# A decoder layer on one core: latents, queries, keys and values computed span by span inside the tail program

## What is computed

```python
h = rmsnorm(x)                                   # width 1024
b_g, c_g, x_in, q_lat, kv_lat, kr_raw, gate_c, gate_a = split(h @ w_in)
conv_y = short_conv(c_g * x_in)                  # width 512, 3 taps
# latents and queries: the part that is moved
ckv = rmsnorm(kv_lat); kr = apply_rope(rmsnorm(kr_raw))          # 256 and 32 wide
q   = rmsnorm(q_lat) @ w_uq                                      # 384 -> 8 heads x 96
qn  = rmsnorm(q[..., :64]); qr = apply_rope(rmsnorm(q[..., 64:]))
kn  = rmsnorm(ckv @ w_uk); v = ckv @ w_uv                        # 8 heads x 64
# the rest
attn = softmax(qn.kn + qr.kr) @ v
x = x + (sigmoid(gate_c) * (b_g*conv_y) @ w_conv_out + sigmoid(gate_a) * attn @ w_attn_out) @ w_mix_out
h = rmsnorm(x)
# PEER: 8 heads, 2 x 128 keys each, top 16 of the pairs -> 128 experts (of 16384) per token
a = gelu(sum(u[eidx] * h)); x = x + sum(softmax(best) * a * v[eidx])
```

## Time and profile before

| | us |
|---|---|
| median of the runs (3914.68 to 3929.59) | 3915.71 |
| profiled execution: its own time | 3925.3 |
| profiled execution: its span, first to last instruction | 3923.5 |
| latent and query stage (from 46.6 to 370.0) | 323.4 |
| span 0 in the tail (370.0 to the first gather at 719.3) | 349.3 |
| gathers of span 0, beside the work of span 1 (to 1526.6) | 807.3 |
| gathers of span 1, beside the work of span 2 (to 2627.4) | 1100.8 |
| gathers of span 2, beside the work of span 3 (to 3824.1) | 1196.7 |
| gathers of span 3 | 99.4 |

### The profile page before, as it was taken

How to read it: one execution, slowest core, us unless ns; L and a number is a source line. 1 busy time by engine, 2 the same in 40 slices (tenths; PEclk the granted TensorE clock), 3 DMA queues, 4 the chain that set the end, 5 groups by cost and what they waited for, 6 DMA issues and landing times.

```text
span 3923.5 us, 36349 instructions
## 1 busy us (share of the span) xinstructions
PE 3260.3 (83%) x10704; PEld 1824.9 (47%) x10704; DVE 2617.0 (67%) x5677; ACT 1405.3 (36%) x4207; POOL 1120.7 (29%) x1252
## 2 busy tenths in 40 slices
PE   6797898488999987777888899877788887787887
PEld 4423787245555443344544454423444444575431
DVE  1364117777757996777687779964777676756874
ACT  1122201485123233666522233333454444222343
POOL 0000001333323333333333334342333333323442
PEclk9897799788999999888899999998888988676899
DMA  2112243699999989999999999998898888999999
GB/s 92 33 36 67 91 150 102 259 399 404 397 364 408 363 316 372 411 407 406 376 426 426 426 414 378 377 389 344 325 368 350 338 360 336 391 401 412 425 421 385
DMA packets 234020, 1289.23 MB, mean 329 GB/s; under 512 B 45468, under 2 KB 59868, under 8 KB 98341
## 3 DMA queue, kind: packets, MB, share of 16 engines
q0 software_dynamic: 152064, 1107.36, 69.5%
q1 hardware_dynamic: 80036, 175.22, 12.6%
q10 hardware_dynamic: 1728, 4.39, 0.3%
HBM read 1273.47 MB, written 13.40 MB: 328 GB/s over the span
## 4 chain that ended last, share of the span: by engine, by line
PE 35%; DMA 27%; DVE 16%; ACT 5%; issue 5%; POOL 1%; SPq 1%; ACTq 0%; DVEq 0%; POOLq 0%
DMA tl_uv<-in_uv,tl_idx 23%; PE tl_y L905 12%; PE tl_f L1151 6%; DVE tl_uv L1490 3%; PE tl_f L1131 3%; PE tl_f L1162 3%; DVE tl_acc L1477 2%; PE tl_f L1177 2%; DMA X<-in_krope 2%; PE tl_f L965 1%; PE tl_f L1075 1%; PE tl_f L1098 1%; DVE tl_eq L1574 1%; POOL tl_uv L837 1%; PE tl_f L1017 1%
## 5 line engine op out<-in xcount | busy, mean ns | idle before, releaser
L1490 DVE CUSTOM_DVE_ANT_0 tl_uv<-tl_uv,tl_h 128x1024 f32<-128x1024 f32 x1056 | 1272.4, 1217 | 706.4 <-DMA tl_uv<-in_uv,tl_idx 680.4
L837 POOL DMA_INDIRECT tl_uv<-in_uv,tl_idx x1056 | 1042.4, 987 | 1941.1 <-PE tl_y L905 1378.7
L905 PE MATMUL tl_y<-tl_uv,tl_diag 128*128 128x512 f32 (+1 forms) x2552 | 1318.6, 659 | 254.9 <-ACT tl_diag L1198 254.8
L905 PEld LDWEIGHTS tl_y<-tl_uv,tl_diag 128*128 128x128 f32 (+1 forms) x2552 | 491.0, 204 | 916.5 <-issue 497.9
L1226 ACT ACTIVATE tl_ge<-tl_a 128x1 f32<-128x1 f32 x1056 | 209.0, 198 | 1248.1 <-DVE tl_a L1490 1246.5
L1477 DVE SCALAR_TENSOR_TENSOR tl_acc<-tl_uv,tl_w,tl_acc 128x1024 f32<-128x1024 f32 x410 | 524.9, 1280 | 67.2 <-ACT tl_w L1210 66.5
L1210 ACT ACTIVATE tl_w<-tl_ge,tl_weight 128x1 f32<-128x1 f32 x1024 | 301.5, 294 | 33.2
L849 POOL TENSOR_TENSOR tl_cand<-tl_tv 128x48 f32<-128x48 f32 (+5 forms) x128 | 66.1, 544 | 784.2 <-DVE tl_ti L1522 626.1
L1151 PE MATMUL tl_f<-H,w_tail 128*128 128x384 f32 (+2 forms) x1024 | 266.0, 417 | 11.6 <-DMA w_tail<-in_w_merge 7.7
L1177 PE MATMUL tl_f<-H,w_tail 128*128 128x384 f32 (+2 forms) x1024 | 265.8, 414 | 10.2 <-DVE H L1717 9.6
L1198 ACT ACTIVATE tl_diag<-K,tl_w 128x128 f32<-128x128 f32 (+1 forms) x638 | 253.6, 397 | 34.4 <-PE tl_y L905 14.1
(11 more groups left out here) (213 smaller groups left out, 3119.4 us busy)
## 6 DMA issues: line engine op xcount, KB each, us to landing
w_tail<-in_w_merge SPq DMA_DIRECT2D x96, 512.0 KB, 7.6
w_tail<-in_w_peer SPq DMA_DIRECT2D x64, 576.0 KB, 7.7
w_tail<-in_w_conv SPq DMA_DIRECT2D x48, 512.0 KB, 7.9
tl_uv<-in_uv,tl_idx POOLq DMA_INDIRECT x1056, 11.4
w_tail<-in_w_mix SPq DMA_DIRECT2D x32, 512.0 KB, 7.6
X<-in_cache SPq DMA_DIRECT2D x64, 128.0 KB
X<-in_x SPq DMA_DIRECT2D x8, 536.0 KB, 6.9
o_y<-tl_acc ACTq DMA_DIRECT2D x8, 512.0 KB, 6.3
```

The costliest lines, as they stand in the source:

```text
L837: pool.indirect_dma_start(UV[:, u % RING, :], None, d["uv"], bass.IndirectOffsetOnAxis(ap=which, axis=0)).then_inc(landed[u % RING], 16)
L905: mm = pe.matmul(Y[0:m, half * 512:(half + 1) * 512], DG[:, (pe_count[u] - 1) % DIAGS, 0:m], UV[:, u % RING, D + half * 512:D + (half + 1) ...
L1490: dve.tensor_tensor_reduce(UV[:, u % RING, 0:D], UV[:, u % RING, 0:D], HP[:], 1.0, 0.0, ALU.mult, ALU.add, A[:, t % 2, i:i + 1]).then_inc( ...
```

## The change

`latent_stage` and `query_stage` are gone, with the loads ahead of them. Their work stands at the head of each span in `tail_stage`, for that span's tokens alone (272, 384, 384, 32; the meta tokens go with span 0):

- `project(c)`: the six latent blocks for the span's tokens, as six more groups of the weight ring (fetched again in each span), the sums of squares by matmul, roots, reciprocals, scaling and RoPE of KR.
- `questions(c)`: for each tile of 128 tokens (and once for the meta tokens) queries, keys and values with tokens on the partitions. Then a head's sum of squares is a DVE reduction along the free axis, and its reciprocal root a number per token and head, used straight from SBUF. The matmuls for sums and spreads of the query stage go; transposes of q and k by PE (per tile 16 of them) come in, because attention wants channels on the partitions. `w_uq`, `w_uk` and `w_uv` are loaded in each span, the first two into the weight ring's space.
- Queries, keys and values of a tile are still stored to HBM, tile by tile, and attention of the same span reads them back after waiting for these stores.
- The `TICK` table gets entries for the new steps (8 ticks each, for 8 + 3 x tiles + 2 steps; 6 for span 3's projection), so units are spread over them too.
- The samples' absorbed queries stay in SBUF, and the decode's loads are issued a little later in the span.

The core of the diff (removed functions and equal edits of offsets left out):

```diff
-                            norm_stage(nc, "n1_", X, H, K, d["g_mix"], w_lat, x_dram=d["x"])
-                            latent_stage(nc, H, K, CQ, CKV, KR, CS, w_lat, w_head, out_kept, d)
-                        query_stage(nc, K, CQ, CKV, KR, CS, QABS, QRS, w_head, out_kept, d)
+                norm_stage(nc, "n1_", X, H, K, d["g_mix"], w_tail, x_dram=d["x"])
                 tail_stage(nc, K, X, H, w_tail, d)
...
         for c in range(NCH):
+            order += [(c, LATENT, b) for b in range(4)] + [(c, LSUM, 0), (c, LATENT, 4), (c, LATENT, 5), (c, LSUM, 1), (c, LSUM, 2)]
+            for z in range(len(steps[c])):
+                order += turn_groups(c, z - 1) * (z > 0)
+                order += [(c, QP, 2 * z), (c, QP, 2 * z + 1)] * asks(c, z) + [(c, KP, z), (c, VP, z)] * keeps(c)
...
-        PRE = [len(x) + 5 + NCV for x in items] + [DEC + NCV]
-        TICK = [[6 + 2 * PARTS[c][1]] * len(items[c]) + [8] * 5 + [8] * NCV
+        BODY = [len(x) + 5 + NCV for x in items] + [DEC + NCV]
+        ASK = [3 * len(x) + 2 for x in steps]
+        PRE = [BODY[c] + ASK[c] + NLT + 2 for c in range(NCH)]
+        TICK = [[8] * (NLT + 2) + [8] * ASK[c]
+                + [6 + 2 * PARTS[c][1]] * len(items[c]) + [8] * 5 + [8] * NCV
...
@@ SyncE
+            def ask_loads(c):
+                p0, n = lat_span[c]
+                sp.wait_ge(proj, ready[c, LATENT, NLT - 1])
+                sp.dma_start(WQ, d["w_uq"]).then_inc(wq_in, 16)
...
+                    sp.dma_start(WK, d["w_uk"]).then_inc(wq_in, 16)
+                    sp.dma_start(WV[:], d["w_uv"]).then_inc(wq_in, 16)
...
+                for z, (lo, m, t) in enumerate(steps[c] if keeps(c) else []):
+                    sp.wait_ge(act_took, act_count[c, KTR, 2 * z + 1])
...
+                        sp.dma_start(d["s_q"][:, :, t * P:(t + 1) * P].rearrange("h p n -> p h n"), QTT[:]
+                                     ).then_inc(q_stored, 16)
+                    sp.dma_start(d["s_k"][:, :, at:at + m].rearrange("h p n -> p h n"), KTT[:, :, 0:m]).then_inc(q_stored, 16)
...
             def attention_loads(c, a, n):
-                if c:
-                    sp.wait_ge(proj, ready[c - 1, SCORE, HC - 1])
-                    sp.wait_ge(ranked, c)
+                sp.wait_ge(lat_stored, 32 * (c + 1))
+                sp.wait_ge(q_stored, 16 * kept(c + 1, 0))
...
@@ TensorE
+            def project(c):
...
+                for b in range(NLT):
+                    units(due(c, b - PRE[c], 0))
...
+                    for k in range(KD):
+                        mm = pe.matmul(F[0:m, bank_of[c, LATENT, b], 0:n], W[:, s, k, 0:m], H[:, k, p0:p0 + n],
+                                       start=(k == 0), stop=(k == KD - 1))
...
+            def ask(c, z):
+                lo, m, t = steps[c][z]
+                if z == 0:
+                    pe.wait_ge(wq_in, 16 * (3 * c + (3 if keeps(c) else 1)))
+                    pe.wait_ge(lat_set, c + 1)
...
+            def ask_turn(c, z):
+                m = steps[c][z][1]
+                if asks(c, z):
+                    pe.wait_ge(q_norm, asked(c, z) + 1)
...
+            def questions(c):
+                n, at = len(steps[c]), ASK[c] + BODY[c]
+                for z in range(n + 1):
+                    units(due(c, 3 * z - at, 0))
+                    if z:
+                        ask_turn(c, z - 1)
+                    if z < n:
+                        ask(c, z)
...
@@ ScalarE
+            def ask_root(c, z):
...
+                act.wait_ge(q_ss, at_step(c, z) + 1)
+                ins = act.activation(QRT[0:m, a:b], QSS[0:m, a:b], ACT.Sqrt, bias=K[0:m, C_EPS:C_EPS + 1], scale=1.0 / NOPE)
...
@@ VectorE
+            def project(c):
+                n, at = lat_span[c][1], 8 * c
+                units(due(c, NLT - PRE[c], LAG_DVE))
...
+                dve.wait_ge(lat_root, c + 1)
+                for i, (b0, b1) in enumerate(((0, QT), (QT, QT + KT), (QT + KT, NLT))):
...
+                    dve.reciprocal(r, r).then_inc(lat_step, 1)
+                    dve.wait_ge(lat_step, at + i + 1)
+                    for b in range(b0, b1):
+                        x = LQ[:, b, 0:n] if b < QT else LC[:, b - QT, 0:n] if b < NLT - 1 else LR[:, 0:n]
+                        ins = dve.scalar_tensor_tensor(x, x, GLAT[0:m, b:b + 1], r, ALU.mult, ALU.mult)
...
+            def questions(c):
+                at = ASK[c] + BODY[c]
+                for z in range(len(steps[c])):
+                    units(due(c, 3 * z - at, LAG_DVE))
+                    ask_squares(c, z)
+                    units(due(c, 3 * z + 1 - at, LAG_DVE))
+                    ask_scale(c, z)
```

More of the change, by code:

```diff
@@ L501, in start, with load @@
         sp.dma_start(self.tile[:, s, 0:src.shape[1], :], src).then_inc(self.arrived[s], 16)
+    def load(self, sp):
+        for w in range(WRING):
+            self.start(sp, w)
 def tail_stage(nc, K, X, H, weights, d):
```

727 lines of the change are left out of this document (351 added, 376 removed).

## The result

The changed kernel takes 3952.77 us (median of 7 runs, 3948.66 to 3962.62), the kernel before 3917.11 in the same series (7 runs, 3914.68 to 3932.64): a ratio of 1.0088, 95% interval [1.0069, 1.0106]. It is slower by 0.9%, where the prediction said 2.0% faster. The profiled execution has a span of 3955.5 us against 3923.5.

The account below looks back on a forecast made before the run. Engines one by one bound it before the first gather; after, engines in span 1, DMA in span 2. 3923.5 - 240 + 89 + 42 + 30 = 3844.5, + 1.8 - 9.6, said 3836 us; over all cases 3750 to 3898.

Parts of the forecast that it names:

- The front: Up to the first gather: two stages of 323.4 us go, 89 us of work comes back; 240 us earlier.
- Bytes: Traffic added beside the units in spans 1 and 2: 8.6 MB, 20 us, or 26 with small stores at half rate.
- Span 1: Gather 0 to 256: new steps cost 153 us, 52 returned elsewhere, 12 at the stream's start; net +89 us.
- Span 2: Gather 256 to 640: new steps cost 150 us, units moved out of old ones return 108; net +42 us.
- the DMA needs 47 x 2.43 + 26 = 140: it sets the pace: Span 2's new steps: 47 units at 2.43 us plus 26 us of bytes exceed PE's 124 us; 140 us.
- returned 47 units at 2.3: 108: Span 2's old stretches: 47 units now stand in new steps, each giving back 2.3 us; 108 us.
- 8 buffers (19 us of gathers) cover waits of 6 to 13 us: Span 2's new steps: landed gathers outlast PE's waits, so DMA keeps the pace; 19 us of gathers.
- Span 3: Gather 640 to 1024: new steps cost 87 us, less 20 units at 2.5 and 7 at the start; net +30 us.
- The table loads: On ACT, ten more roots between GELUs bring 20 loads of 1.28 us, 26 us, costing nothing beyond the chains' counted loads.
- the 3862: Whole-kernel time if each table load on ACT also drained about 1.38 us, 28 us more; left out of the sum.
- A: Only bytes count beside the units: added PE and DVE work finds room, 64 us come back, 3740 us; 17%, below 3785.
- B: New steps: ring closes, units hide nothing, serial length 347 us, 4023 us; decides from 240 exposed; 9%, above 3935.

Follow-up runs that it names:

- experiment 2: Kernel before, with 17 extra DRAM-to-DRAM copies (8.8 MB) in each of spans 1 and 2 and no engine work: 3957.11 us, ratio 1.0111.
- Experiment 1: Kernel before, with 20/25 in place of 23/25 of the units beside span 2's work spread over it, no new steps: 3966.54 us, ratio 1.0134.
- experiment 7: Changed kernel, with no units in the new steps of spans 1 to 3: 3956.38 us, ratio 1.0112.
- experiment 8: Changed kernel, with 24 ticks in place of 8 ahead of the first tile and of attention: 3920.70 us; with 48: 3926.77 us.
- experiment 10: Spread share 24 of 25 for 23: kernel before 3932.18, changed 3894.97, changed with gathered units 3857.67 us; 25 of 25: before 3937.49, gathered 3891.16.
- experiment 3: Changed kernel, with attention of spans 1 and 2 reading an input without waiting for the stores, which are still made: 3950.48 us, ratio 1.0093.
- experiment 4: Changed kernel, with q, k, v of spans 1 and 2 not stored and attention reading an input: 3927.52 us, ratio 1.0024.
- experiment 5: Changed kernel, storing values in rows of 2 KB: 3954.66 us; storing q, k and v in rows of 2 to 4 KB: 3964.0 us.

## Why the prediction was wrong

**The front** was right: 240 us forecast, 242 measured (scores at 135.5 for 136, first gather at 477.3 for 479).

**Bytes** were right in size: 20 us a span forecast for the bytes as such, 19.2 and 20.5 measured in experiment 2. The 6 more a span for stores in small pieces at half rate stay untested as a rate.

**Span 1** came out nearly right, +100 for +89, in part because two errors of its halves met: the new steps cost 21 us more than I said, the old ones gave back 10 more. TensorE's work fits (107.8 us for 109). The wait before attention is 20.4 us where I had 13; those for the latents (10.8 for 13) and ahead of the transposes (6.2, 5.0 and 5.7 for 6 each) fit.

**Span 2 is the step that failed:** "the DMA needs 47 x 2.43 + 26 = 140: it sets the pace" and "returned 47 units at 2.3: 108". Measured are 63 us returned, 45 less. The price of 2.43 is right where units stand alone and was carried to where they stand beside work, because the stretch had a DMA share of 0.98 and its merge 1.01. A share near 1 does not say how far the time falls when units leave. Experiment 1 shows this without the change (1.4 us a unit), experiment 7 from the other side (1.7 us in either place). These are averages over some 40 units; single changes of place gave from 0 to 4.0 us a unit (experiments 8 and 10), and what sets the price stays open. The new steps cost 31 us more than forecast, because the DMA did not set their pace (share 0.85) and the waits did: "8 buffers (19 us of gathers) cover waits of 6 to 13 us" and "10 at attention's start". The sum left 26 us for waits (150 less 124 of TensorE's work); TensorE waits 59, of which 24.2 are at attention's start and 15.7 for the latents. The store and the load are held up by the gathers that the ring has under way (experiments 3 to 5 and 7), and the stores of the two spans cost 25 us (experiment 4).

**Span 3**: the new steps cost 77 us where I had 80, and returned 23 where I had 50. By the trace 18 dot products moved, for the 20 units forecast, so a unit gave back 1.3 us and not 2.5. No experiment was made on this span alone.

**The table loads** are 20 more (166 for 146) and 1.28 us each, as counted, and behind 142 of the 166 the next instruction starts within 0.1 us. ACT's timeline in the changed kernel has such a pair, the load of GELU's table and GELU.

```profile
1520.06 1.28 ACT L1088 ACT_TABLE_LOAD   x1
1521.36 0.20 ACT L1088 ACTIVATE tl_ge<-tl_a 128x1 f32<-128x1 f32 x1
```

The drain that the Trainium skill puts on a load ("ScalarE: Activation LUTs", section "What ACT_TABLE_LOAD costs") does not show here either. No run moved the roots, so their effect on the time was not tried. (The recorded 3834, from which the 3862 is counted, should be the 3836 of the sum.)

**The rivals.** A fell: it gave 3740, and the waits and TensorE's work came on top of its bytes. B, the slower end, named the right mechanism (the ring closes while TensorE waits, and what is moved hides nothing) with a condition of 240 us exposed, and gave 4023. The time lies between it and my forecast, and among what I had put down to B, all above 3935, with a chance of 9%. Its own sign, waits over 25 us at every tile, did not show: those at the tiles are 5 to 7 us. My rule for it, "no unit moves in the new steps and no time is returned elsewhere", was too strict: without units there experiment 7 has the same time as the changed kernel, and its new steps take 120 and 130 us where I had 136. The measured 3953 lies outside my range, which ended at 3898. The sign I gave for span 2, a DMA share of 0.96 or more, failed as well: it is 0.94.

**What stays open.** How far the units' exact places matter beside their share: 24 of 25 gained 58 to 63 us in the changed kernel and 25 of 25 only 30, and the price of a unit in span 2 runs from 0 to 4.0 us; no run tells places from share. Which engine holds the old steps where the DMA does not was not tried either. That the read-back could be avoided by keeping the first heads in SBUF was not tried.

## What to carry to other kernels

A busy share near 1 gives no price: before work is priced by the resource that looks full, take a few units of it out of the stretch and see what they give back. Here 44 units out of a stretch with a share of 0.99 gave back 6% of its time, 1.4 us each for 2.4 alone. When a change alters how much work a stretch holds, the numbers that spread background work over it must be fitted again before it is judged: here the changed kernel was 0.9% slower than the kernel before with the old share and 0.6% faster with the next one. And ahead of a dependent store and load, count what is already in the DMA queues, not the landing time at rest.

## What the runs showed of the hardware

Beside gathers of 8 KB pieces, a store of 256 KB in pieces of 256 B, issued behind two others, landed 21.3 us after its issue, and without gathers beside it 5.0 us. In rows of 2 KB it landed after 22.2 us with q and k ahead of it still in small pieces, and after 11.4 us with these in large rows too, both beside gathers. An issue on SP's queue was itself held 14.01 us behind such stores, and took 0.33 us without them, so a load can be late though it waits for nothing.
